# Score maxima of grouped-query attention on two halves of the array, and output weights split early and kept in DRAM

## The chip, the cores and the metric
The kernel runs on one core of one Trainium2 chip. The metric is the time of one execution on the device in microseconds (us), lower is better. The engines are TensorE (PE, with its weight loads as PEld), VectorE (DVE), ScalarE (ACT), GpSimd (POOL) and SyncE (SP), whose queue issues the transfers.

## The reference
One transformer layer over 1,024 tokens (a grid of 16 rows by 64 columns) of width 1,024, with 256 context tokens of which only keys and values are used. After a modulated RMS norm, a projection feeds three mixers: a long convolution (hyena, 256 wide), grouped-query attention (8 query heads on 2 key/value heads, 64 wide, over 1,024 + 256 keys) and attention in a neighbourhood of 8 by 16 (4 heads). Their outputs pass an output projection, and a gated feed-forward layer follows. All of it is float32. The part that matters here:

```python
q_l = apply_rope(rms_norm(q_l, qk_g_q[l]), cos, sin)
k_l = apply_rope(rms_norm(k_l, qk_g_k[l]), cos, sin)
gqa_l = gqa_latent(q_l, jnp.concatenate([k_c, k_l], axis=1), jnp.concatenate([v_c, v_l], axis=1))
    # in it: s = einsum(q, k) * ATTN_SCALE; p = softmax(s); o = einsum(p, v)
na_l = natten_latent(nq_l, nk_l, nv_l, nk_c, nv_c, na_rpb[l])
mix_l = jnp.concatenate([hyo_l, gqa_l, na_l], axis=-1) @ w_out[l]
```

## The kernel before
Every float32 operand of a product is split into a high and a low float16 part, and the product is made of high times high, high times low and low times high. The engines' programs are written by hand; the order of each engine's instructions is the order in the code, and semaphores join them. All transfers are issued by SP, in the order of its program.

**Projection stage.** 28 units (`UNITS`): 10 of kind 2 (neighbourhood keys and values), 10 of kind 1 (grouped-query keys and values, neighbourhood queries), 8 of kind 0 (grouped-query queries). `GROUP0[g]` is the first unit of a kind: 0, 10 and 20. For each unit TensorE runs `project(u)` and then `turn_qk(u - 2)`, the transposes of the unit two back. ScalarE reads the product (`from_psum`), makes the high parts (`hi_parts`) and copies the transposes (`turned`). VectorE runs `slot(u)`: mean square, rotation of unit u - 1, scaling of u (L2654, L2663), low parts of u - 1 (L2694), and then `meanwhile(u)`, which among others takes one row of the late modulation chunks (`late_row`, L2505) in each of the units 8 to 15. GpSimd makes the inverse roots (L1093). `turn_qk(u)` waits for the low parts of u (`pr_lo`). Weights arrive in chunks (`CHUNKS`) in four slots of 8 KB per partition; `load(c)` waits until the chunk that had the slot is used. Chunks 33 to 36 are the last four late ones, and follow chunk 32, the fourth of kind `qkv`. In the units 6 and 7 the hyena output is made and split (L2629, semaphore `y_rdy`, 4 in all).

**Neighbourhood stage.** 32 attention units, pipelined; among them the query units of kind 0 are projected, and the first eleven of the grouped-query maximum chunks (`early_chunk`) run in banks that are free for a while. The column of a query head in `qT` holds the high part in partitions 0 to 63 and the low part in 64 to 127; `kT[:, kv, 0]` holds the high part of the keys twice, `kT[:, kv, 1]` the low part and ones.

**Grouped-query stage.** 16 groups (8 blocks of 128 tokens by 2 key/value heads) of 10 steps, one for each tile of 128 keys. A step computes scores transposed, keys by 4 heads of 128 queries, with two matmuls of 512 columns (`step_scores`); the second takes `q2`, whose lower half is the high queries again (copied by GpSimd, `high_queries`, L1061) and whose upper half is the shift of each query, so that the exponential can be taken at once. ScalarE takes the exponential twice, as float16 (L2094) and as float32 (L2097); the difference is the low part, made by VectorE (L2810) for 6 tiles of a group and by GpSimd (L1077) for 4, for one of which GpSimd also makes the float16 part (L1075). Nine small matmuls weigh the values four steps later. For the shifts, a separate pass computes the plain scores of the group to come: 10 chunks (4 heads by 2 halves of the keys, and 2 for the context) of 512 columns, `chunk(c)` on all 128 partitions, one in each step, 13 steps ahead, in two banks by turns; VectorE takes the maximum of each (L2786), and at the tenth the negated maximum of all (L2799). TensorE moves it into place (`turn_shifts`, step 8) and ScalarE copies it (L2086).

```python
ps, k = PS[:, chunk_bank(c)], kT[:, c.kv, 0]
ins = mm(ps, qT[:, GROUP * c.kv + c.i // 2, tok(c.t)], k[:, o:o + 512], True, True)
```

**Output weights.** Four chunks of 1 MB, loaded during the neighbourhood and grouped-query stages; GpSimd scales them (L1047) and splits them (L1051, L1056), in pieces of 512 columns between its other work there. At the start of the grouped-query stage SP waits for the last neighbourhood unit (`o_mm`), then loads x again (3 MB), and, once the weights are split, eight blocks of 256 KB of the feed-forward weights. These loads so far start at 454.8 and later.

## Time and profile before
| | us |
|---|---|
| median of 3 runs | 1267.82 (1267.33 to 1268.02) |
| the profiled execution | 1269.27 |
| its span | 1267.5 |
| TensorE busy | 1242.6 (98%) |
| VectorE busy | 905.6 (71%) |
| ScalarE busy | 648.1 (51%) |
| GpSimd busy | 345.2 (27%) |

All times in the rows are us from the start of the span of the profiled execution. The projection stage reaches to about 293, the neighbourhood stage to about 388, the grouped-query stage to about 550. An engine's busy share is the mean over stages with different limits. An instruction's duration holds its way through the engine; what it costs in a stream is the distance to the next start.

### The profile page before, as it was taken

How to read it: one execution, taken by the hardware profiler on the slowest of the kernel's cores; microseconds unless marked ns; L12 is line 12 of the kernel's file. 1: busy time of each engine (PE TensorE's matmuls, PEld its weight loads, DVE VectorE, ACT ScalarE, POOL GpSimd, SP SyncE). 2: the span in 40 equal slices, each digit the busy share in tenths (PEclk: the TensorE clock that was granted, in tenths of full speed). 3: DMA queues.
4: the chain of work that ended last, by engine and by line, in shares of the span. 5: the costliest groups of instructions: out<-in, count | busy, mean ns of one | idle time of the engine just before them, and what ended most of it. 6: DMA issues, size and time to landing. Idle time of an engine off the chain costs nothing. (4 is left out here: it accounts for less than half of the span.)

```text
span 1267.5 us, 22616 instructions
## 1 busy us (share of the span) xinstructions
PE 1242.6 (98%) x7808; PEld 655.8 (52%) x7808; DVE 905.6 (71%) x1510; ACT 648.1 (51%) x1236; POOL 345.2 (27%) x341
## 2 busy tenths in 40 slices
PE   8999999999999999999999999999999999999997
PEld 1564656556675666664454444444444444444443
DVE  3879886766778999964458866666666675566587
ACT  2532224557779999973135654444454543312424
POOL 0100000114678899850003222333332220000001
PEclk9999999999999999999999999999999999999999
DMA  9628812335210120121130332222223305997963
GB/s 360 266 83 316 288 45 87 113 84 151 68 35 1 35 104 29 33 85 50 50 89 12 92 92 75 81 67 67 76 89 91 91 18 156 332 331 264 344 231 133
DMA packets 108164, 158.89 MB, mean 125 GB/s; under 512 B 8384, under 2 KB 67264, under 8 KB 106816
## 3 DMA queue, kind: packets, MB, share of 16 engines
q1 hardware_dynamic: 108096, 158.00, 36.8%
q8 instruction: 41, 0.67, 0.2%
q14 instruction: 27, 0.22, 0.1%
HBM read 135.95 MB, written 19.93 MB: 123 GB/s over the span
## 5 line engine op out<-in xcount | busy, mean ns | idle before, releaser
L1206 PE MATMUL PS<-arena 128*128 128x512 f16 (+9 forms) x7208 | 1201.1, 327 | 16.0 <-DMA arena<-in_w_mod 5.5
L1206 PEld LDWEIGHTS PS<-arena 128*128 128x128 f16 (+3 forms) x7208 | 604.7, 102 | 586.5 <-issue 39.5
L2894 DVE SCALAR_TENSOR_TENSOR arena<-arena 128x512 f16<-128x512 f32 x148 | 120.9, 823 | 76.6 <-ACT arena L2182 76.6
L2182 ACT ACTIVATE arena<-arena 128x512 f16<-128x512 f32 x140 | 87.6, 629 | 130.4 <-PE PS L1206 130.4
L2786 DVE TENSOR_REDUCE arena<-PS 128x1 f32<-128x512 f32 (+1 forms) x160 | 106.4, 680 | 9.1 <-PE PS L1206 9.1
L2294 ACT ACTIVATE arena<-arena 128x512 f16<-128x512 f32 x77 | 48.2, 629 | 123.3 <-DVE arena L3045 74.2
L2094 ACT ACTIVATE arena<-PS 128x512 f16<-128x512 f32 x140 | 88.3, 631 | 1.2 <-PE PS L1206 0.7
L1173 POOL TENSOR_TENSOR arena<-arena 128x512 f32<-128x512 f32 x20 | 26.6, 1334 | 222.2 <-DMA arena<-in_w_ffn_in 194.0
L1077 POOL TENSOR_TENSOR arena<-arena 128x512 f16<-128x512 f32 x64 | 74.1, 1159 | 9.4 <-ACT arena L2097 8.1
L1200 POOL TENSOR_TENSOR arena<-arena 128x1 f32<-128x1 f32 x8 | 4.7, 598 | 236.0 <-DVE arena L3186 236.0
L2810 DVE TENSOR_TENSOR arena<-PS,arena 128x512 f16<-128x512 f32 x96 | 65.4, 681 | 4.0 <-ACT PS L2097 3.9
L3060 DVE SCALAR_TENSOR_TENSOR arena<-arena 128x512 f16<-128x512 f32 x77 | 52.1, 686 | 20.2 <-ACT arena L2294 20.2
L2936 DVE TENSOR_TENSOR arena<-PS,arena 128x512 f32<-128x512 f32 x60 | 41.3, 688 | 32.4 <-PE PS L1206 31.2
L2097 ACT ACTIVATE PS<-PS 128x512 f32<-128x512 f32 x96 | 60.5, 632 | 0.0
L3045 DVE TENSOR_TENSOR arena<-arena 128x512 f32<-128x512 f32 x44 | 30.2, 690 | 37.7 <-DMA arena<-in_w_ffn_out 32.7
L2970 DVE TENSOR_TENSOR arena<-arena 128x512 f16<-128x512 f32 (+1 forms) x77 | 51.5, 683 | 0.0
L1119 POOL MEMSET arena<- 128x128 f16 x2 | 0.4, 205 | 181.7 <-PE PS L1460 181.7
L2245 ACT CAST arena<-arena 128x512 f16<-128x512 f32 (+1 forms) x77 | 44.9, 607 | 5.0 <-DVE arena L2977 2.9
L2217 ACT COPY arena<-PS 128x512 f32<-128x512 f32 x60 | 34.4, 576 | 18.4 <-PE PS L1206 18.4
L2097 ACT ACTIVATE arena<-PS 128x512 f32<-128x512 f32 x64 | 41.3, 646 | 0.0
L2222 ACT ACTIVATE arena<-arena 128x512 f32<-128x512 f32 x40 | 24.9, 623 | 28.3 <-DVE arena L2936 28.3
L2756 DVE CUSTOM_DVE_ANT_0 PS<-PS,arena 128x640 f32<-128x640 f32 x32 | 26.6, 831 | 16.9 <-PE PS L1206 16.4
(204 smaller groups left out, 1156.8 us busy)
## 6 DMA issues: line engine op xcount, KB each, us to landing
arena<-in_w_ffn_out SPq DMA_DIRECT2D x121, 256.0 KB, 5.1
arena<-in_w_mod SPq DMA_DIRECT2D x23, 1024.0 KB, 7.4
arena<-in_w_ffn_in SPq DMA_DIRECT2D x88, 256.0 KB, 3.0
arena<-in_w_in SPq DMA_DIRECT2D x9, 1024.0 KB, 5.5
left_operands<-arena SPq DMA_DIRECT2D x33, 256.0 KB, 2.2
arena<-left_operands SPq DMA_DIRECT2D x3, 2816.0 KB, 11.7
arena<-lay_bias SPq DMA_DIRECT2D x12, 512.0 KB, 4.0
arena<-in_x SPq DMA_DIRECT2D x2, 2048.0 KB, 13.9
```

The costliest lines, as they stand in the source:

```text
L1077: pool.tensor_tensor(pt[:, 1], Pf[s.full], pt[:, 0], ALU.subtract).then_inc(pt_lo2, 1)
L1206: return pe.matmul(out, lhsT, rhs, start=start, stop=stop, skip_group_check=True)
L2094: act.activation(Pt[s.s % RING_P][:, 0], PS[:, s.bank], ACT.Exp)
L2097: act.activation(Pf[s.full] if s.by_pool else PS[:, s.bank], PS[:, s.bank], ACT.Exp).then_inc(s_exp, 1)
L2182: act.activation(aS[n % RING][:, 0], weight_block(p, b), ACT.Copy, scale=WS).then_inc(blk_hi, 1)
L2245: act.copy(dst, f_op[name]).then_inc(fi_hi, 1)
L2294: act.activation(foS[q % FO_RING][:, 0], src, ACT.Copy, scale=WS).then_inc(fo_hi, 1)
L2786: dve.tensor_reduce(out, ps, AX, ALU.max).then_inc(s_max, 1)
L2810: dve.tensor_tensor(pt[:, 1], PS[:, s.bank], pt[:, 0], ALU.subtract).then_inc(pt_lo, 1)
L2894: dve.scalar_tensor_tensor(dst[:, 1], src, WS, dst[:, 0], ALU.mult, ALU.subtract).then_inc(blk_lo, 1)
L2970: dve.tensor_tensor(dst[:, 1], f_op[name], dst[:, 0], ALU.subtract).then_inc(fi_lo, 1)
L3060: dve.scalar_tensor_tensor(foS[q % FO_RING][:, 1], src, WS, foS[q % FO_RING][:, 0], ALU.mult, ALU.subtract).then_inc(fo_lo, 1)
```

## The change
1. **Maxima on half arrays, in pairs.** For odd heads `qT` now holds the low part in partitions 0 to 63 and the high part in 64 to 127. The maximum pass takes the high queries alone: one head on partitions 0 to 63, the other on 64 to 127, as two matmuls of 64 rows into two banks (`Pair`, five a group, one in every second step, banks 4 and 5 each time). VectorE takes one maximum over 1,024 columns for a pair. The first ten chunks, in the neighbourhood stage, stay single, on one half each; the eleventh goes.
2. **Shifts.** The negated maximum is split into a float16 part and its rest: three dependent VectorE instructions in place of one.
3. **High queries by transfer.** Since odd heads have them in the other half, SP issues two transfers a group in place of GpSimd's copy: groups 0 and 1 during the bias loads, the others after the loads of the feed-forward blocks.
4. **Tiles.** GpSimd makes the low part of 5 tiles of a group in place of 4, and the float16 part of 3 in place of 1.
5. **Output weights.** Eight pieces of 512 KB are loaded, scaled by GpSimd, split by ScalarE (high) and GpSimd (low), 1,024 columns an instruction, one in each unit from 11 on, and stored in DRAM; at the start of the grouped-query stage they are loaded back, 4 MB, ahead of x. The fourth late modulation sum moves in two steps to make room.
6. TensorE's loop over the groups is written out.

```diff
-LEAD, LAG, SHIFT_AT, SEND_AT = 13, 4, 8, 4
+LAG, SHIFT_AT, SEND_AT, LEAD = 4, 8, 4, 6
-RING_P, RING_F = 5, 4
-POOL_TILES, CAST_TILE, LAST_CASTS = (1, 4, 6, 8), 4, (0, 3, 5, 7)
-CHUNK_BANK, STEP_BANK, OUT_BANK = (5, 1), (0, 2, 4, 3), (6, 7)
+RING_P, RING_F = 5, 5
+POOL_TILES, CAST_TILES, LAST_CASTS = (1, 3, 5, 7, 9), (1, 3, 7), (0, 4, 8)
+NPAIR_G = 5
+PAIR_BANK, STEP_BANK, OUT_BANK = (4, 5), (0, 2, 1, 3), (6, 7)
...
+    def pairs(self):
+        if self.s < 2:
+            return [Pair(NPAIR_G + self.s)] if self.s else []
+        return [Pair(self.s // 2 + LEAD, self.it)] if self.s % 2 == 0 and self.s // 2 + LEAD < NGROUP * NPAIR_G else []
...
+        def query_heads(kv, h, t):
+            rows = slice(HD * (h % 2), HD * (h % 2) + HD)
+            return qT[rows, GROUP * kv + h, tok(t)], kT[rows, kv, 0]
...
+            def load_wo(h):
+                k, n = 4 * (h // 4) + 2 * (h % 2), h // 2 % 2
+                sp.dma_start(wo_raw[h % 2], w_out[:, k:k + 2, 512 * n:512 * n + 512]).then_inc(wo_raw_in[h % 2], 16)
+            def keep_wo(h):
+                sp.wait_ge(wo_split, h + 1)
+                if h + 2 < N_WO:
+                    load_wo(h + 2)
+                sp.dma_start(wo_kept[:, h // 2, :, 2 * (h % 2):2 * (h % 2) + 2], wo_parts[h % 2])\
+                    .then_inc(wo_out[h % 2], 16)
...
                     load(c, w_in[:, kh:kh + 4, col:col + 512], (4, 512))
+                if c == chunk_index("qkv", 3):
+                    sp.wait_ge(y_rdy, 4)
+                    for h in range(2):
+                        load_wo(h)
...
+            def high_queries(g):
+                s = Step(NKT * g)
+                if g >= 2:
+                    sp.wait_ge(st_mm, NKT * (g - 1))
+                for b in range(2):
+                    high = qT[HD * b:HD * b + HD, GROUP * s.kv + b:GROUP * s.kv + GROUP:2, tok(s.t)]
+                    dst = q2[s.kv][0:HD].rearrange("p (h b t) -> p h b t", b=2, t=P)[:, :, b]
+                    sp.dma_start(dst, high).then_inc(q2_hi[s.kv], 16)
...
             sp.wait_ge(o_mm, NNA)
+            sp.wait_ge(pr_r, n_normed(NU - 1))
+            for n in range(4):
+                sp.dma_start(woS[n], wo_kept[:, n]).then_inc(wo_in, 16)
             for i in range(3):
                 sp.dma_start(x1[:, 2 * i:2 * i + 2], x_rows[:, 2 * i:2 * i + 2]).then_inc(x1_in, 16)
...
             for b in range(2):
-                sp.wait_ge(wo_split, 3 + b)
                 for a in ("A11", "A12", "A21", "A22"):
                     load_fi(a, 0, b)
+            sp.wait_ge(pr_tc, NU)
+            for g in range(2, NGROUP):
+                high_queries(g)
...
+            def wo_scale(h):
+                pool.wait_ge(wo_raw_in[h % 2], 16 + 16 * (h // 2) + 16)
+                r = flat(wo_raw[h % 2])
+                pool.tensor_scalar(r, r, WS / HS if h in (0, 2) else WS, None, ALU.mult).then_inc(wo_scaled, 1)
+            def wo_low(h):
+                pool.wait_ge(wo_hi, 3 + h + 1)
+                pool.tensor_tensor(flat(wo_parts[h % 2][:, 1]), flat(wo_raw[h % 2]), flat(wo_parts[h % 2][:, 0]),
+                                   ALU.subtract).then_inc(wo_split, 1)
...
                 inverse_roots(u)
+                h = u - GROUP0[1] - 1
+                if h >= 1:
+                    wo_low(h - 1)
+                if 0 <= h < N_WO:
+                    wo_scale(h)
...
+            def pair(p):
+                if p.p == NPAIR_G:
+                    pe.wait_ge(pr_n, n_normed(NU - 1))
                     pe.wait_ge(pr_tc, NU - 1)
                 else:
+                    pe.wait_ge(s_max, n_paired(p) - 1)
+                for o in range(2 if p.i == NPAIR_G - 1 else 1):
+                    for b in range(2):
+                        if p.i == NPAIR_G - 1:
+                            q, k = query_heads(p.kv, 2 * o + b, p.t)
+                            ins = mm(PS[:, PAIR_BANK[b], C * o:C * o + C], q, k[:, S:S + C], True, True)
+                        else:
+                            q, k = query_heads(p.kv, 2 * (p.i // 2) + b, p.t)
+                            ins = mm(PS[:, PAIR_BANK[b]], q, k[:, 512 * (p.i % 2):512 * (p.i % 2) + 512], True, True)
                 ins.then_inc(s_mm, 1)
...
+            def wo_high(h):
+                act.wait_ge(wo_scaled, 3 + h + 1)
+                if h == 1:
+                    act.wait_ge(late_used, 24 + LATE_MOVE + 1)
+                elif h >= 2:
+                    wo_stored(act, h - 2)
+                act.copy(flat(wo_parts[h % 2][:, 0]), flat(wo_raw[h % 2])).then_inc(wo_hi, 1)
...
-                dve.tensor_reduce(maxima, mx[:, c.kv], AX, ALU.max, negate=True).then_inc(sh_rdy, 1)
+                dve.tensor_reduce(lowest, mx[:, c.kv], AX, ALU.max, negate=True).then_inc(sh_rdy, 1)
+                dve.wait_ge(sh_rdy, 3 * c.g + 1)
+                dve.tensor_copy(maxima, lowest).then_inc(sh_rdy, 1)
+                dve.wait_ge(sh_rdy, 3 * c.g + 2)
+                dve.tensor_tensor(rest_of_maxima, lowest, maxima, ALU.subtract).then_inc(sh_rdy, 1)
```

## Rows read from the trace of the kernel before

**Rows 1.** Busy time of each engine in three stretches, number of instructions, granted clock, transfers.
```profile
core 0: us, PE busy (x) PEld busy (x) DVE busy (x) ACT busy (x) POOL busy (x), PEclk, DMA share, GB/s
250.00:260.00 10.00, 10.00 (x54) 4.80 (x53) 6.98 (x23) 7.25 (x15) 1.39 (x2) 1.00 0.01 3
340.00:360.00 20.00, 19.91 (x232) 14.39 (x230) 15.71 (x40) 15.00 (x36) 13.52 (x12) 1.00 0.19 54
460.00:480.00 20.00, 19.61 (x239) 12.94 (x236) 18.63 (x35) 19.90 (x41) 18.94 (x21) 1.00 0.54 210
```
**Rows 2.** TensorE's timeline, grouped-query stage: start, length, what, wait before.
```profile
410.98 1.18 PE L1206 MATMUL PS<-arena 128*128 128x512 f16 x12 [0.19 <-ACT arena L2086]
...
454.27 10.41 PE L1206 MATMUL PS<-arena 128*128 128x512 f16 x126 [0.20 <-ACT arena L2086]
464.86 10.39 PE L1206 MATMUL PS<-arena 128*128 128x512 f16 x126 [0.18 <-ACT arena L2086]
```
**Rows 3.** VectorE's timeline, two score maxima in a row.
```profile
467.89 1.29 DVE L2786 TENSOR_REDUCE arena<-PS 128x1 f32<-128x512 f32 x2
```
**Rows 4.** TensorE's timeline, filter taps on 64 rows (L1206) between transposes (L1276).
```profile
42.25 1.12 PE L1206 MATMUL PS<-arena 64*128 64x512 f32 x2
43.30 0.66 PE L1276 MATMUL PS<-arena 128*128 128x128 f32 x4
43.89 1.39 PE L1206 MATMUL PS<-arena 64*128 64x512 f32 x4
45.21 0.66 PE L1276 MATMUL PS<-arena 128*128 128x128 f32 x4
```
**Rows 5.** Groups of instructions by shape, 15 to 62, float32 passes of 512 columns.
```profile
L1206 PE MATMUL PS<-arena 128*2 128x512 f32 x50 | 22.1, 592 | 0.0
```
**Rows 6.** TensorE's timeline, projection stage: a turn, and a unit's product.
```profile
235.21 0.61 PE L1460 MATMUL PS<-arena 128*128 128x128 f16 x8
...
238.72 5.34 PE L1206 MATMUL PS<-arena 128*128 128x512 f16 x24
```
**Rows 7.** VectorE's timeline, units 7 to 9.
```profile
229.69 1.31 DVE L2629 TENSOR_TENSOR arena<-arena 128x512 f16<-128x512 f32 x1 [0.19 <-ACT arena L1965]
...
231.76 0.74 DVE L2518 TENSOR_SCALAR arena<-arena 128x1024 f32<-128x1024 f32 x1
233.03 0.43 DVE L2654 SCALAR_TENSOR_TENSOR arena<-PS,arena 128x256 f16<-128x256 f32 x1 [0.53 <-ACT arena L1987]
233.54 0.69 DVE L2694 TENSOR_TENSOR arena<-arena 128x512 f16<-128x512 f32 x1
```
**Rows 8.** SP's timeline: the four late chunks, first to last issue.
```profile
203.31 13.98 SPq L811 DMA_DIRECT2D arena<-in_w_mod  x4
```
**Rows 9.** Transfers by line, us to landing: the first, and the last two, of these.
```profile
arena<-in_w_mod SPq DMA_DIRECT2D x1, 1024.0 KB, 5.1
...
arena<-in_w_mod SPq DMA_DIRECT2D x2, 1024.0 KB, 8.2
```
**Rows 10.** Groups by shape, GpSimd, 220 to 560: busy, mean ns, idle before.
```profile
L1077 POOL TENSOR_TENSOR arena<-arena 128x512 f16<-128x512 f32 x64 | 74.1, 1159 | 9.4 <-ACT arena L2097 8.1
L1047 POOL TENSOR_SCALAR arena<-arena 128x512 f32<-128x512 f32 x16 | 23.8, 1494 | 0.0
...
L1075 POOL CAST arena<-arena 128x512 f16<-128x512 f32 x16 | 9.8, 615 | 9.7 <-ACT arena L2097 9.7
```
**Rows 11.** GpSimd's timeline, the last query's rotation.
```profile
391.05 1.27 POOL L1109 TENSOR_TENSOR arena<-arena 128x512 f32<-128x512 f32 x1
```
**Rows 12.** What TensorE waited for, 420 to 430: total, times, longest.
```profile
PE PS L1206 <- POOL arena L1077: 1.0, 1, 1.0
```
**Rows 13.** Transfers by line, us to landing: issues from 1123.4 to 1124.8.
```profile
arena<-left_operands SPq DMA_DIRECT2D x1, 2816.0 KB, 10.0
...
arena<-in_w_ffn_out SPq DMA_DIRECT2D x1, 256.0 KB, 11.8
```
**Rows 14.** TensorE's timeline, its last matmuls.
```profile
1251.78 8.37 PE L1206 MATMUL PS<-arena 128*128 128x512 f16 x38
```
**Rows 15.** Busy time and granted clock (0.76) after them.
```profile
1264.00:1265.00 1.00, 0.00 (x0) 0.00 (x0) 0.00 (x0) 0.00 (x0) 0.00 (x0) 0.76 1.02 379
```

More of the change, by code:

```diff
@@ L74, in n_split @@
 def n_split(c):
-    return sum(k not in AS_IS and k != "wo" for k in CHUNKS[:c + 1])
+    return sum(k not in AS_IS for k in CHUNKS[:c + 1])
 STEPS = [(p, b) for p in ("P2", "P1", "P5", "P6", "P7", "P3", "P4") for b in range(2)]
@@ L818, in _ @@
             n_of["mod"] = 1
-            for c in range(1, N_EARLY):
+            for c in range(1, len(CHUNKS)):
                 if c == 1:
@@ L1618, in step @@
                 step_scores(s)
-                for c in s.chunks():
-                    chunk(c)
+                for p in s.pairs():
+                    pair(p)
                 if s.turns_shifts():
@@ L1674, in _ @@
             weigh(Unit(NNA - 1))
-            for s in range(3, BODY):
+            for s in range(3, NSTEPS):
                 step(Step(s))
@@ L2007, in turned @@
                 if g == 0:
+                    if t == 0:
+                        for h in range(N_WO - 2, N_WO):
+                            wo_stored(act, h)
                     ins = act.copy(qT[:, :, tok(t)], ps)
@@ L2816, in step @@
             def step(s):
-                for c in s.chunks():
-                    chunk_maximum(c)
+                for p in s.pairs():
+                    pair_maxima(p)
                 if s.s:
```

231 lines of the change are left out of this document (108 added, 123 removed).

## The prediction
> **What bounds the kernel now.** I read the windows first, one for each stage that the change touches [rows 1]. Where TensorE is busy throughout, a microsecond by which it is late is, as a rule, a microsecond of the kernel. In the projection stage (250 to 260) TensorE is full, VectorE and ScalarE have some 30% free and GpSimd does almost nothing. In the neighbourhood stage (340 to 360) TensorE is full but for 0.09 of 20 us. In the grouped-query stage (460 to 480) ScalarE is as full as TensorE, VectorE has 7% left and GpSimd 5%.
>
> Then the timeline of TensorE in that last stage: a beat of 10.59 us for each group of ten steps (454.27 to 464.86), with one wait of 0.2 us at its start, for the shifts that ScalarE copies at L2086 [rows 2]. The reader is to see that both engines run at their limit: ScalarE has 21 instructions a group, 0.50 each, and is busy for 19.90 of 20 us; TensorE is idle only where it waits for ScalarE. A 512-column matmul costs it 0.216 us in a stream ((5.34 - 0.38) / 23, where 0.38 is the length of one, in [rows 6]). The wait and the restart behind it leave 10.24 us of its own work in a group. VectorE starts its 512-column instructions 0.61 apart (1.29 for two of 0.68) [rows 3]: 16 of them are 9.8 us, plus small ones. ScalarE sets the beat; TensorE and VectorE are a few per cent behind.
>
> **The change, part by part.**
> *Grouped-query steps.* ScalarE loses two float16 exponentials a group, 0.50 each: 10.6 - 1.0 = 9.6 us. TensorE loses ten 512-column matmuls (2.16 us) and gets five pairs at P each. VectorE has 5 low parts (3.0), 5 maxima over 1,024 columns and some more small ones. Two 512-column ones end to end are 1.22, so I take 1.15 each, with one start in place of two, and 0.8 for the shift's chain of three and the reciprocal: 9.6 us. GpSimd has 5 low parts at 1.16, 3 casts at 0.61 and the outputs (some 1.2), in place of a scaling or two, a split and a copy more than it keeps: 8.8 us [rows 10]. Everything hangs on P. The trace has no float16 matmul on 64 rows; the nearest are the float32 taps [rows 4]. A float32 pass of 512 columns costs about 0.43 (22.1 us for 50, 0.44) [rows 5]. Two passes on one half, from 42.25 to the next start at 43.30, take 1.05, where streaming wants 0.86. The four passes of 128 columns behind them take 0.59 to the next start, where 0.44 is the stream (0.11 each, a quarter of 0.43). So one visit to the half array costs 0.19 + 0.15 = 0.34 us beside its work. Four passes, two on each half, take 1.32 where one half alone would need 1.72: the halves do overlap, the second adding 0.27 to the first's 1.05. For float16, whose weights are half as wide, I take 0.22 for the stream, 0.05 for the second half's later start and 0.23 for the two changes of shape, P = 0.50, between 0.40 (0.18 of changes only) and 0.65 (all 0.34 and some weight loading). A group is then 10.24 - 2.16 + 2.5 + 0.1 (the two semaphore waits at its start remain) = 10.7 on TensorE, 0.1 more than now: the saving of two heads at once goes into changing shape ten times a group. Over 15 groups +1.5 us, from -6 (P 0.40) to +13 (0.65).
> The Trainium skill's page "TensorEngine Tiling (Array Packing)", section "Key Properties", says that a change of tiling mode, not just of tile, drains TensorE. It gives no price; the 0.34 us of the taps is what a drain each way looks like here.
>
> *Early chunks, neighbourhood stage.* Ten of them now run on one half each. Each costs a visit (0.2 to 0.34) and saves nothing; TensorE is full there, less a wait of 0.25 in every four units that can absorb some. Chunk 10 leaves (0.22). +1.2 us (0 to +3).
>
> *The weights' loads ahead of the projection stage.* The queue of SP now waits, behind the load of the fourth projection chunk, until the hyena output is split, and only then goes on to the four late modulation chunks. That split ends at 231.0 (229.69 + 1.31, [rows 7]). Now the four are issued from 203.3 to 217.3 [rows 8], and the first is read at 231.76, 0.8 us after the point where its load may start in the new kernel. Ahead of it go two loads of 512 KB. A 1 MB load lands 5.1 us after issue on an empty queue, and a fourth in a row after some 9 (8.2 is the median of the last two), so each MB adds 2 to 2.6, of which I take 2.6 [rows 9]. 231.1 + 5.1 + 2.6 = 238.8: VectorE stands 7.0 us at L2518. Queued behind it are the scaling (L2654) and low part (L2694) of the units that follow; now they end 1.2 us after the one at 233.03 begins [rows 7]. In the new order they end at 238.8 + 0.7 + 1.2 = 240.7, and TensorE's turn of that unit, now at 235.21 [rows 6], waits for them: 5.5 us. TensorE is full before and after, so nothing gives it back. I take +5.7 (4 to 7).
>
> *Splitting on GpSimd and ScalarE.* GpSimd gets a scaling and a subtraction over 1,024 columns in each of eight units. From 1.49 and 1.16 for 512 [rows 10]: 2.95 + 2.25, plus the inverse root of 0.70 (1.39 for two in [rows 1]) and about 0.5 of waiting for ScalarE's high part between them, 6.4 us. A unit lasts 5.6 (24 matmuls and the turn of 0.61, less overlap, [rows 6]). GpSimd falls 0.8 us further behind in each of some seven units, to 5.5; what waits for its inverse root (scaling, low parts, turn) has some 2.5 of slack. +3 us (0 to 5).
>
> *GpSimd in the grouped-query stage.* The extra weight work in the third group, for which TensorE waited 1.0 us [rows 12], goes: -1.0. The cast of tile 1 now stands ahead of the last low parts of the queries: +0.6, but inside the stall that follows. Copying the high queries on GpSimd goes too, off the path.
>
> *High queries by DMA.* Groups 0 and 1 are loaded early. Those of group 2 are queued on SP behind everything that now starts at about 392.4, when the last query is rotated (391.05 + 1.27, [rows 11]) and the last unit weighed: 4 MB of split weights, 3 MB of x and eight quarter blocks, 9 MB. At 5.1 for the first MB and 2.6 for each further one they have landed after 25.9 us, at 418.4, and the small loads just behind. Is it one line? A load of 2,816 KB took 10.0 us, and one of 256 KB issued a microsecond behind it took 11.8 [rows 13], where 1 MB on an empty queue takes 5.1 [rows 9]: yes. Group 2 begins at 410.98 [rows 2]. TensorE stands for 419 - 411 = 8 us with ScalarE and VectorE behind it, less the 0.6 above. +7.5 (5 to 10). Group 3 finds its queries landed.
>
> *The clock.* Nothing in the middle of this kernel is long enough to show it; at the end the last matmul is done at 1260.2 (1251.78 + 8.37, [rows 14]) and the granted clock still averages 0.76 from 1264 to 1265, so that it falls from 2.4 to 1.2 GHz some 4.3 us after the last matmul [rows 15]. Two stalls of 5.5 and 7.5 may each be followed by some us at 1.2 GHz. +1 (0 to 4).
>
> Sum: 1.5 + 1.2 + 5.7 + 3 - 1 + 7.5 + 1 = 18.9 us. The profiled execution took 1269.27 us (span 1267.5), 1.45 over the median of 1267.82. 1288.2 on its basis, **1286.7** on that of the median.
>
> **Rivals.**
> *The halves cost no change of shape.* Then P is 0.22 to 0.27, TensorE has 9.3 us a group, and VectorE and ScalarE set the beat at 9.6: -1.0 in each of 15 groups in place of +0.1, 16.5 us less: 1270. For it: the overlap in [rows 4], and the gaps there stand beside float32 weights and waits for VectorE. Against: every one of the changes seen has them. The Trainium skill's page "TensorE: Matmul & The Clock Gate", section "Measured speedup vs the span model", has packed tiles take one matmul plus about 4 ns for each further tile, which would be this rival; the 0.27 of the second half here is more.
> *A load does not block.* If the high queries pass the 9 MB, or those land in a third less time, 7.5 us go: 1279. If the late chunks' rows are not the gate: 1281. Against it the 11.8 us.
> *Faster than before.* The first rival together with the absence of one of the two stalls, say the queries in time: 1286.7 - 16.5 - 7.5 = 1262.7. It decides where P is under 0.27 and group 2 is not kept waiting more than 4 us.
> *Worse.* P at 0.65 or over: 1298 and more.
>
> **How the numbers follow.** My forecast with both stalls and P near 0.50 has 0.50 (its own range 1280 to 1294). One stall missing 0.13, the halves free with both stalls 0.14, both (faster) 0.17, P high 0.06. A change within 0.2%, 2.5 us, is about what a measurement cannot tell from none: 0.04 of the cases end there. Faster 0.16, same 0.04, slower 0.80. The range from 1268 to 1298 leaves out the faster cases and the worst.
>
> **What would show it.** In the new profile: a hole of about 7 us in VectorE before the first late row (now L2518), released by a DMA, and one of 5.5 in TensorE; TensorE's beat at 10.6 to 10.8 us, with gaps around each pair; the two matmuls of a pair starting within 0.06 us; a hole of some 8 us at the start of group 2, released by the DMA of the high queries; ScalarE no longer full. I am wrong if the beat is 9.6 to 9.8, if the first pair follows its neighbours without a gap, or if either hole is missing.

## The result and the profile after

The changed kernel takes 1304.09 us (median of 4 runs, 1303.27 to 1304.67), the kernel before, measured beside it, 1267.62: a ratio of 1.0287, 95% interval 1.0269 to 1.0305, slower by 36.5 us. The profiled execution took 1304.67 us, its span is 1302.9, 35.4 more than before. 1286.7 was forecast, 1268 to 1298 the range. The sign was right, and both stalls and the beat of a group came where they were expected; the loss was twice the size that was forecast.

The windows of the changed kernel in the three stretches of [rows 1]:

```profile
250.00:260.00 10.00, 10.00 (x54) 4.76 (x53) 7.27 (x16) 4.45 (x11) 7.55 (x8) 1.00 0.60 185
340.00:360.00 20.00, 19.82 (x217) 13.53 (x214) 15.16 (x41) 13.93 (x35) 10.83 (x10) 1.00 0.22 61
460.00:480.00 20.00, 19.07 (x238) 10.87 (x239) 18.71 (x27) 18.56 (x37) 15.86 (x20) 1.00 0.04 8
```

ScalarE is no longer full, as forecast. But no engine is full in the last stretch: something small is waited for in each group.

To see where 35.4 us come from, I put the two traces side by side at fixed points of TensorE's order (the transposes of a unit, the scores of a step) and took the difference, less the difference at unit 7, which lies ahead of every edit. The same for some of the experiments told below, in us behind the kernel before:

```
point                  after    e1     e2     e3     e5    e10    e16
unit 9                   8.0   0.0    8.7    7.3    7.4    0.0    0.0
unit 17                 15.1   7.1   13.1   14.4   10.3    0.0    0.0
unit 19                 16.8   8.8   19.5   16.1   13.4    4.6    4.6
unit 25                 20.2  14.2   22.1   18.3   18.6    7.9    5.5
step 18 (group 1)       22.2  15.8   24.3   20.2   20.8    7.8    5.6
step 28 (group 2)       33.6  28.0   35.4   20.4   32.1    7.8    5.4
step 38                 32.6  27.1   34.4   19.4   31.1    6.6    4.1
step 140                34.6  29.1   36.4   21.4   33.2    6.5    3.1
last matmul             35.5  30.0   37.3   22.3   34.1    7.5    3.3
```

The first column is the account of the loss: 8.0 to unit 9, 8.8 in units 11 to 19, 3.4 in the neighbourhood stage, 2.0 in the first steps, 11.4 at group 2, 1.0 given back in group 3, 2.0 in the groups behind it, 0.9 at the end. Some 6.7 us of it are TensorE's clock, which fell four times; they are told below.

The first hole, on VectorE's timeline, then TensorE's (the same places before: [rows 6, 7]):

```profile
239.09 0.75 DVE L2581 TENSOR_SCALAR arena<-arena 128x1024 f32<-128x1024 f32 x1 [7.34 <-DMA arena<-in_w_mod]
```
```profile
240.83 1.03 PE L1498 MATMUL PS<-arena 128*128 128x128 f16 x8 [5.53 <-DVE arena L2757]
```

7.0 and 5.5 were forecast. The turn behind it takes 1.03 us, not 0.61. The windows say why:

```profile
236.00:238.00 2.00, 0.00 (x0) 0.00 (x0) 0.00 (x0) 0.00 (x0) 0.00 (x0) 1.00 1.02 387
238.00:239.00 1.00, 0.00 (x0) 0.00 (x0) 0.00 (x0) 0.00 (x0) 0.00 (x0) 0.90 1.02 418
239.00:240.00 1.00, 0.00 (x0) 0.00 (x0) 0.92 (x2) 0.00 (x0) 0.00 (x0) 0.50 1.04 430
...
244.00:245.00 1.00, 1.00 (x6) 0.75 (x5) 1.00 (x2) 0.00 (x0) 0.00 (x0) 0.50 1.05 410
245.00:246.00 1.00, 1.00 (x8) 0.76 (x7) 0.32 (x1) 0.00 (x0) 0.00 (x0) 0.69 0.97 385
246.00:247.00 1.00, 1.00 (x14) 0.84 (x12) 0.27 (x1) 0.45 (x2) 0.11 (x1) 1.00 1.05 393
```

TensorE stops at 235.3; the granted clock falls to half (1.2 GHz) from about 238.8 (a mean of 0.90 in 238 to 239) and stays there until about 245.6 (0.69), nearly five us into the new work. That costs another 2.3 us.

The second hole, SP's timeline and TensorE's:

```profile
414.00 1.94 SPq L960 DMA_DIRECT2D arena<-split_output_weights  x4
415.98 1.56 SPq L962 DMA_DIRECT2D arena<-in_x  x3
417.58 20.59 SPq L967 DMA_DIRECT2D arena<-in_w_ffn_in  x8
438.27 2.54 SPq L924 DMA_DIRECT2D arena<-arena  x4
```
```profile
442.54 3.85 PE L1242 MATMUL PS<-arena 128*128 128x512 f16 x24 [9.04 <-DMA arena<-arena]
```

The high queries of group 2 are the last line of SP: they are not even issued before 438.27, since issuing eight loads of 256 KB took SP 20.59 us behind 7 MB. Another 2.3 us go to the clock here too: it is down from 436.8 to 447.0, 4.5 us into the new work.

The clock fell twice more, and no long hole stands before these falls. The first comes behind the turn of unit 16: TensorE's next 46 matmuls in the changed kernel, then in run 6 below, whose program is the same up to the grouped-query stage, then the granted clock of the changed kernel:

```profile
291.04 9.33 PE L1242 MATMUL PS<-arena 128*128 128x1 f32 x46
```
```profile
291.12 7.65 PE L1242 MATMUL PS<-arena 128*128 128x1 f32 x46
```
```profile
293.00:294.00 1.00, 1.00 (x8) 0.53 (x7) 0.58 (x2) 1.00 (x4) 0.86 (x1) 0.71 0.68 147
294.00:295.00 1.00, 1.00 (x4) 0.34 (x3) 1.00 (x1) 0.70 (x3) 1.00 (x1) 0.50 1.02 338
...
413.00:414.00 1.00, 1.00 (x18) 0.91 (x17) 1.00 (x2) 0.00 (x0) 1.00 (x1) 0.50 0.00 0
```

The clock is at 1.2 GHz from 293.4 to 296.8, with TensorE at work, and costs 1.7 us (9.33 less 7.65). In the ten us before, TensorE had stood twice, for 1.23 and 1.16 us. Run 6 stands for 1.15 us in the same place and keeps its clock, so that one execution has such a fall and another has not. The fourth fall, from 412.9 to 416.3, follows waits of 1.26, 1.70 and 0.79 us in the first steps of the grouped-query stage. There other waits take up most of it: run 1, which has no fall there, loses 1.6 us from unit 25 to step 18, the changed kernel 2.0.

Units 11 to 19, where the largest miss lies; VectorE and GpSimd in unit 14:

```profile
274.01 2.53 DVE L2757 TENSOR_TENSOR arena<-arena 128x128 f16<-128x128 f32 x2 [0.44 <-ACT arena L2044]
```
```profile
273.09 2.13 POOL L1115 TENSOR_TENSOR arena<-arena 128x1024 f16<-128x1024 f32 x1
275.19 2.81 POOL L1111 TENSOR_SCALAR arena<-arena 128x1024 f32<-128x1024 f32 x1
```

The two low parts of the keys took 0.63 together before (0.29 and 0.42, one behind the other):

```profile
268.65 0.63 DVE L2694 TENSOR_TENSOR arena<-arena 128x128 f16<-128x128 f32 x2 [0.38 <-ACT arena L2000]
```

Now the first ends at 275.37, when GpSimd's subtraction ends (275.22), and the second takes 1.25 beside the next. GpSimd meanwhile is idle 1.4 to 1.6 us a unit: it is not behind, as I had it; it is in the way. The Trainium skill, "SBUF — State Buffer", section "Who interferes with whom", has the rule: VectorE and GpSimd share a pair of ports under an exclusive lock; a VectorE instruction with two inputs in SBUF is blocked by a GpSimd instruction that reads SBUF until that one ends, one with a single input is not, and some copies and scalings take the pair too. The trace agrees, with 0.63 against 2.53. Of the 8.8 us, 1.7 are the fall of the clock at 293.4; 7.1 are left.

The grouped-query stage, TensorE [rows 2] and the chain it waits for:

```profile
464.46 10.28 PE L1242 MATMUL PS<-arena 128*128 128x128 f16 x126 [0.47 <-DVE arena L2877]
475.21 0.96 PE L1242 MATMUL PS<-arena 128*128 128x128 f16 x14 [0.47 <-DVE arena L2877]
```
```profile
474.14 0.17 DVE L2873 TENSOR_REDUCE arena<-arena 128x4 f32<-128x12 f32 x1
474.34 0.26 DVE L2875 CAST arena<-arena 128x4 f16<-128x4 f32 x1
474.51 0.61 POOL L1125 CAST arena<-arena 128x512 f16<-128x512 f32 x1
...
474.63 0.52 DVE L2877 TENSOR_TENSOR arena<-arena 128x4 f16<-128x4 f32 x1
```

The beat is 10.75 us. A pair: the last full matmul ahead of one starts at 476.80, both halves at 477.11 (0.003 apart), the next full one at 477.43: 0.63, less 0.22 for the full one, P = 0.42 us. And a subtraction on four columns takes 0.52: it ends at 475.15, with GpSimd's cast (475.12).

### The profile page after: what moved, and what is told of

It is laid out like the page before. It is cut to its first block, busy times and chain, and to the rows that moved or that the text cites. A ratio compares the mean times of both kernels' runs of the same rounds, so it can differ in the third digit from the quotient of the medians.

```text
span 1302.9 us, 22186 instructions
## 1 busy us (share of the span) xinstructions
PE 1252.1 (96%) x7808; PEld 641.5 (49%) x7808; DVE 920.6 (71%) x1450; ACT 646.7 (50%) x1213; POOL 362.4 (28%) x341
## 4 chain that ended last, share of the span: by engine, by line
PE 61%; DVE 8%; issue 2%; SPq 2%; ACT 2%; POOL 1%; DMA 1%; another core or an unknown queue 0%; DVEq 0%; POOLq 0%; ACTq 0%
PE PS L1242 59%; SPq L967 2%; DVE arena L2862 1%; PE PS L1560 1%; DMA arena<-weight_sum_rows 1%; DVE arena L3207 1%; DVE arena L3210 1%; DVE arena L3087 1%; DVE arena L2969 1%; PE PS L1312 1%; ACT arena L2397 1%; POOL arena L1127 1%; DVE arena L3077 1%; DVE arena L2877 0%; ACT arena L2055 0%
## 5 line engine op out<-in xcount | busy, mean ns | idle before, releaser
L1242 PE MATMUL PS<-arena 128*128 128x512 f16 (+10 forms) x7208 | 1209.3, 329 | 32.2 <-DMA arena<-arena 9.0
L1242 PEld LDWEIGHTS PS<-arena 128*128 128x128 f16 (+4 forms) x7208 | 590.6, 102 | 625.1 <-issue 47.3
L2862 DVE TENSOR_REDUCE arena<-PS 128x2 f32<-128x1024 f32 (+1 forms) x75 | 91.6, 1222 | 20.1 <-PE PS L1242 17.7
L1127 POOL TENSOR_TENSOR arena<-arena 128x512 f16<-128x512 f32 x80 | 92.4, 1156 | 23.9 <-ACT arena L2154 20.1
L2151 ACT ACTIVATE arena<-PS 128x512 f16<-128x512 f32 x109 | 65.7, 603 | 18.5 <-PE PS L1242 18.1
L2888 DVE TENSOR_TENSOR arena<-PS,arena 128x512 f16<-128x512 f32 x80 | 54.4, 680 | 3.7 <-ACT PS L2154 3.6
L2154 ACT ACTIVATE arena<-PS 128x512 f32<-128x512 f32 x80 | 47.7, 597 | 3.2 <-PE PS L1242 1.6
L2154 ACT ACTIVATE PS<-PS 128x512 f32<-128x512 f32 x80 | 48.7, 609 | 0.0
L2579 DVE SCALAR_TENSOR_TENSOR arena<-arena 128x1024 f32<-128x1024 f32 x28 | 36.6, 1309 | 3.4 <-DMA arena<-in_w_mod 1.6
```

The lines of the kernel that those rows point to most:

```text
L1127: pool.tensor_tensor(pt[:, 1], Pf[s.full], pt[:, 0], ALU.subtract).then_inc(pt_lo2, 1)
L1242: return pe.matmul(out, lhsT, rhs, start=start, stop=stop, skip_group_check=True)
L2151: act.activation(Pt[s.s % RING_P][:, 0], PS[:, s.bank], ACT.Exp)
L2154: act.activation(Pf[s.full] if s.by_pool else PS[:, s.bank], PS[:, s.bank], ACT.Exp).then_inc(s_exp, 1)
L2862: dve.tensor_reduce(out, ps, AX, ALU.max).then_inc(s_max, 1)
L2888: dve.tensor_tensor(pt[:, 1], PS[:, s.bank], pt[:, 0], ALU.subtract).then_inc(pt_lo, 1)
```

## The experiments

Medians of 4 to 7 runs; single runs of one kernel spread by up to 7 us, so differences under 2 us are read from the table and the traces, not from medians. The clock has a part in the spread: the traces of runs 1, 3, 4, 5, 8 and 11 have a fall of 3.4 us near 136, ahead of every edit, and the others have none there. The table leaves that one out, since it counts from unit 7, but not the later ones. Ratios are to the kernel before.

**1. Late chunks first.**

```diff
-                if c == chunk_index("qkv", 3):
+                if c == chunk_index("qkv", 4) - 1:
                     sp.wait_ge(y_rdy, 4)
```

> The changed kernel with one edit: the queue of SP issues the last four late modulation chunks before it waits for the split hyena output, so their loads start some 15 us earlier; the two first loads of the output weights stay behind that wait. Theory (the queue's order starves VectorE): the hole of 5.5 us in TensorE at 235.3 and the 2.3 us that its unit 9 loses at the lower clock behind it both go, the span is 8.0 us shorter, 1296 us. Rival (something else holds the late row, or the hole moves on to the next chunk of weights): at least 4 of the 8 us stay, 1300 or more. If the clock's 2.3 us were not due to the hole they would stay too: 1298.5.

1297.56 us (1.0226, 1.0209 to 1.0243). The hole and the clock's 2.3 us are gone at unit 9, exactly 8.0 us. Of these 2.0 are lost again by unit 25. 1.4 of them go between units 20 and 21, where the clock is down from 320.4 to 323.8 in this run and not in the changed kernel; the other 0.6 go between units 19 and 20, where ScalarE stands for something that the trace does not name. Its waits in the neighbourhood stage (293 to 400), in the changed kernel and here:

```profile
ACT arena L2138 <- remote: 2.7, 1, 2.7
```
```profile
ACT arena L2138 <- remote: 3.3, 1, 3.3
```

The kernel before has no such line; 16 of the 17 kernels derived from the changed one have one, of 1.2 to 4.3 us on ScalarE; run 17 has none. It is open below.

**2. ScalarE does not wait for GpSimd's scaling.**

```diff
-                act.wait_ge(wo_scaled, 3 + h + 1)
+                act.wait_ge(wo_raw_in[h % 2], 16 + 16 * (h // 2) + 16)
...
-                act.copy(flat(wo_parts[h % 2][:, 0]), flat(wo_raw[h % 2])).then_inc(wo_hi, 1)
+                act.activation(..., ACT.Copy, scale=WS / HS if h in (0, 2) else WS).then_inc(wo_hi, 1)
```

> The changed kernel with one edit: ScalarE makes the high part of the output weights from the loaded rows by itself (it scales as it copies) and waits for no one but the load; GpSimd scales and subtracts as much as before, later in the unit. Two theories for the 8.8 us that units 11 to 19 lose. Loop theory (ScalarE waits for GpSimd's scaling, the high parts of keys behind it are late, so VectorE's row and TensorE's turn): without that wait the units are back at 5.6 us, 1295.5 us. Port theory (VectorE's low parts of the keys, 0.29 and 0.42 us alone, take 1.43 and 1.25 beside a scaling or subtraction of GpSimd): GpSimd works as long as before, so the two rows of VectorE stay near 1 us or more each and at least 5 of the 8.8 us stay, 1300 to 1304.

1306.09 us (1.0298, 1.0281 to 1.0315), units 11 to 19 lose 10.7 instead of 8.8: the loop theory, by which they would lose nothing, falls. But the port theory's own sign is only half met: the low parts are back at 0.68 for two. The victim has changed. VectorE's scaling of two columns (0.17 us elsewhere) now meets GpSimd's subtraction, and ends with it (279.85):

```profile
278.11 1.78 DVE L2701 TENSOR_SCALAR arena<-arena 128x2 f32<-128x2 f32 x1
```
```profile
276.88 2.97 POOL L1113 TENSOR_TENSOR arena<-arena 128x1024 f16<-128x1024 f32 x1
```

GpSimd pays as well, 2.97 in place of 2.13, behind VectorE's late rows. The 10.7 us are not all the port's: in this run ScalarE also waits 10.5 us for the stores of the split weights (262 to 300), and the clock is down from 300.5 to 307.4. Up to unit 17, ahead of that fall, 4.4 us are lost, where the changed kernel without its own fall loses 5.4.

**3. Queries between the loads.** SP's order at the end of the neighbourhood stage: queries of group 2, 4 MB of weights, group 3, x, group 4, four blocks, group 5, four blocks, the rest.

> The changed kernel with one edit: the copies of the high queries of groups 2, 3, 4 and 5 stand between the loads of the output weights (4 MB), x (3 MB) and the blocks of the first layer (2 MB) in SP's queue, where they stood behind all of them. Theory (the queue of loads keeps group 2's queries): the hole of 9.2 us at 433 and the 2.3 us at the lower clock behind it go, less what GpSimd's casts had still to catch up: 1304.1 - 11 = 1293. Rival (GpSimd, or the weighing of the last neighbourhood unit, is the gate, the queries land early anyway): no more than 3 us are gained, 1301. Second rival: the hole moves to group 3 or 4, whose queries now follow 4 MB or 3 MB: 3 to 6 us stay, 1296 to 1299.

1292.88 us (1.0194, 1.0177 to 1.0211), 11.2 less. In the table group 2 costs 0.2 in place of 11.4, and no later group is kept waiting by a load.

**4. No half of the array.**

```diff
-            rows = slice(HD * (h % 2), HD * (h % 2) + HD)
+            rows = slice(0, P)
```

> The changed kernel with one edit: every matmul of the maximum pass, early chunks and pairs, uses all 128 rows (high and low parts of the queries against the high keys), so that no half of the array is ever used and the two heads of a pair follow one another. Theory (a pair costs 0.417 us: one stream of 0.216 and 0.20 for two changes of shape, so that it saves next to nothing against two streams of 0.432): the beat of a group goes from 10.75 to 10.82 us, +1.1 over 15 groups, and the ten early chunks give back 0.1 each: 1304 within 1.5 us. Rival (the two halves at once save a whole stream a pair, 0.216, and the rest of the beat is a wait): 75 pairs cost 16 us more, 1320. Rival (the changes of shape cost more than the stream saves): 1300 or less.

1304.29 us (1.0276, 1.0259 to 1.0293): the same time. The beat is 10.86, 0.11 more. Between units 21 and 24 TensorE no longer falls behind (0.00 a unit, where the change loses 0.42 for two early chunks). So a visit to one half costs 0.21 us, and a pair saves 0.02.

**5. GpSimd out of the weights' split.** Experiment 2's ScalarE edit, and on VectorE, at the end of each unit from `GROUP0[1] + 2`:

```diff
+            def wo_low(h):
+                dve.wait_ge(wo_hi, 3 + h + 1)
+                dve.scalar_tensor_tensor(flat(wo_parts[h % 2][:, 1]), flat(wo_raw[h % 2]),
+                                         WS / HS if h in (0, 2) else WS, flat(wo_parts[h % 2][:, 0]),
+                                         ALU.mult, ALU.subtract).then_inc(wo_split, 1)
```

> The changed kernel with one edit: GpSimd no longer touches the output weights; ScalarE makes the high part (scaling as it copies) and VectorE the low part (scale and subtract in one instruction of 1.2 us, as its late rows), at the end of each unit. Port theory (VectorE's low parts of the keys stood still beside GpSimd's weight work): they are back at 0.29 and 0.42 us, a unit back at 5.4 to 5.7 us although VectorE does 1.2 us more in it, units 11 to 19 lose at most 1.5 of the 8.8 us, 1295.5 to 1297. Rival (the whole of the weight work is too much for the stage, whoever does it): VectorE, 70% busy before, becomes the limit, units stay at 6.5 us or more, 1301 or more.

1301.4 us (1.0257, 1.024 to 1.0274). The low parts are back:

```profile
273.70 0.63 DVE L2743 TENSOR_TENSOR arena<-arena 128x128 f16<-128x128 f32 x2 [0.57 <-ACT arena L2029]
```

Units 11 to 17 lose 2.8 where the change loses 7.1, and 1.7 of each are a fall of the clock: 1.1 against 5.4, though VectorE does 1.2 us more in each. But most of it is gone by unit 25: ScalarE now stands for something that GpSimd's slowness had hidden, the stores of the split weights. Of ScalarE's waits, 262 to 300:

```profile
ACT arena L2086 <- DMA split_output_weights<-arena: 10.3, 5, 4.6
```

**6. Shifts after the weighing**: on TensorE `step_weigh` ahead of `turn_shifts`.

> The changed kernel with one edit: in the step where the shifts of the next group are transposed, TensorE first weighs the values of that step (0.57 us) and then transposes, so that VectorE's chain of three small instructions, whose last takes 0.52 us beside a cast of GpSimd, is done by then. Theory (the wait of 0.47 us at each group's shifts is the only thing in which TensorE, 10.2 us of work, is late): the beat goes from 10.75 to 10.25 or 10.3 us, 14 groups give 6.5 us, 1297.5. Rival (ScalarE's copy of the shifts then comes too late for the first step of the next group, or VectorE with its 10.05 us a group takes the limit at once): the beat stays at 10.6 or more, 1302 or more.

1304.01 us (1.0274, 1.0257 to 1.0291), the beat 10.57: 0.17 us of the wait came back. The chain's subtraction still ends with GpSimd's cast (477.86 and 477.82), and TensorE stands twice, 0.17 us each, for it and for the maximum behind it. The 2.4 us that 14 groups give back do not show in the median. In the trace they do (36.9 us behind at step 28, 36.7 at the last matmul, where the changed kernel goes from 33.6 to 35.5), but the clock is down from 324.6 to 331.4 in this run and not in the changed kernel, and takes as much (2.5 us lost from unit 20 to 21, 0.4 in the changed kernel).

**7, 8. The edits 1, 3, 5 and 6 together, and with them the early chunks on all rows.**

> The changed kernel with the edits of the late loads, of the queries' copies between the loads, of the output weights' split on ScalarE and VectorE, and of the shifts after the weighing, all together. If the four losses are separate, they add: 7.2 + 11.2 + 8.8 + 6.5 = 33.7 us less than 1304.1, 1270.4. If one hides behind another (TensorE, once early, waits for the bias tables' loads or for GpSimd): 1274 or more. If removing stalls lets the queries' group or VectorE gain more: 1267.

> As the run with the four edits, and the ten early chunks of the maximum pass in the neighbourhood stage use all 128 rows, while the pairs stay on the two halves. An early chunk on one half costs 0.20 us for its two changes of shape and saves nothing: 10 of them, 2.0 us less than with the four edits alone, 1268.4. Rival (other waits of the stage take it up): no difference, within 0.5 us.

1279.59 (1.0096, 1.0079 to 1.0113) and 1280.17 us (1.0096, 1.0074 to 1.0118). 24.5 of the 33.7 us: not separate, since ScalarE waits 10.4 us for stores here too. The early rows do stop the loss of 0.42 a unit; the median does not show 2 us, the traces 1.7 at the last matmul (9.9 and 8.2 behind).

**9, 10, 11. On top: the high part last in ScalarE's unit; then the first pairs at steps 2, 3, 5, 6; then all pairs on 128 rows.**

> As the run with the four edits and the early rows, and ScalarE makes the high part of the output weights after the high parts of the keys and the copies of the turned tiles, at the end of its unit. Theory (in units 15 to 19 ScalarE stands 10.4 us in all before that copy, until the store of the split weights two halves earlier has landed, and holds up the keys behind it): the keys no longer wait, TensorE has back 2 to 5 of the 5.9 us that it is behind at unit 19, 1275 to 1278. Rival (ScalarE's wait only moves to the next unit's copies out of PSUM, or the copies of the near values gate the next stage anyway): less than 1 us, 1279.5 to 1280.5.

> As the run before it, and the first pairs of the maximum pass come at steps 2, 3, 5 and 6 in place of 1, 2, 4 and 6. Theory (at steps 0 to 3 TensorE waits 2.5 us for VectorE's maxima over 1,024 columns, because all pairs use the same two banks and three of them follow one another within 4 us): 1 to 2 us less than the run with the high part last. Rival (VectorE has its work to do in those steps in any order): no difference within 0.5 us.

> As the run with the pairs spread, and all pairs on 128 rows, so that no half of the array is used anywhere. By the rate of the first such run (0.10 us a group) it is 1.5 us slower than that run, within 1 us. If, with the stalls gone, VectorE alone sets the beat, no difference; if TensorE's switching costs more than it shows, up to 2 us faster.

1277.67 (1.0077, 1.006 to 1.0094), 1274.35 (1.0046, 1.0031 to 1.0061) and 1279.31 us (1.0082, 1.0066 to 1.0099). The first steps lose nothing now (table, e10, unit 25 to step 18). With the stalls gone the halves are worth something: the beat is 10.58 with them and 10.79 without, 0.21 us a group.

**12. The kernel before, with work on GpSimd that nobody uses**, in six units, on a scratch buffer (its results go nowhere):

```diff
                 inverse_roots(u)
+                if GROUP0[1] + 1 <= u <= GROUP0[1] + 6:
+                    extra = f32(104, 1024)
...
+                    own.step(pool.tensor_tensor(extra, extra, extra, ALU.subtract))
+                    own.wait()
+                    own.step(pool.tensor_scalar(extra, extra, 1.0, None, ALU.mult))
```

> The kernel before with work added that nobody uses: in six units of the projection stage (12 to 17) GpSimd, behind its inverse root, subtracts and then multiplies 1,024 columns in a scratch buffer (2.2 and 2.8 us). No wait is added but that the next inverse root comes behind it, which has 5 us to spare. Port theory: VectorE's low parts of the keys, 0.29 and 0.42 us now, take 1.2 us or more each where they fall beside it, and each of the six units is 0.6 to 1.3 us longer: 1268 + 4 to 8 = 1272 to 1276. Rival (the 8.8 us came from the waits between the engines and the stores, not from the port): both rows keep their length, 1268 to 1269.

1272.63 us (1.0032, 1.0021 to 1.0044), 4.0 us behind at unit 17 and 3.7 at the last matmul, with no fall of the clock before that. VectorE before, VectorE here, and GpSimd beside it:

```profile
245.98 0.28 DVE L2694 TENSOR_TENSOR arena<-arena 128x128 f16<-128x128 f32 x1
```
```profile
247.95 1.77 DVE L2703 TENSOR_TENSOR arena<-arena 128x128 f16<-128x128 f32 x1
249.64 2.13 DVE L2525 SCALAR_TENSOR_TENSOR arena<-arena 128x1024 f32<-128x1024 f32 x1
```
```profile
247.68 1.89 POOL L1130 TENSOR_TENSOR arena<-arena 128x1024 f32<-128x1024 f32 x1
249.66 2.78 POOL L1132 TENSOR_SCALAR arena<-arena 128x1024 f32<-128x1024 f32 x1
```

0.28 becomes 1.77 (ending 249.72, GpSimd's 249.57), with no semaphore between the two. That is the collision without the weights, their loads and their stores. One wait came with it: VectorE stood once, 2.4 us, for the inverse root of the first of these units, which GpSimd reached late.

**13. The chain's maxima in PSUM** (on top of 10):

```diff
+        lowest_ps = PS[:, PAIR_BANK[0], 0:GROUP]
...
-                    query_shifts(p)
+                    query_shifts(p, lowest_ps)
...
+                if p.i == 0 and p.p > NPAIR_G:
+                    pe.wait_ge(sh_rdy, 3 * p.g)
```

> As the run with the pairs spread, and VectorE keeps the four maxima of a group in PSUM (in a bank that the pairs use) in place of SBUF, so that the chain's copy and subtraction read PSUM; TensorE's first pair of a group waits for the chain. Port theory: the chain's copy and subtraction, 0.26 and 0.52 us beside GpSimd's cast, take 0.18 each as where GpSimd rests (0.18 and 0.18 in the first group), TensorE's two small waits of 0.17 us a group go, the beat is 10.57 - 0.34 = 10.23 us, 4.5 to 5 us less: 1269.5. Rival (VectorE's own work, 10.05 us a group, or ScalarE sets the beat anyway): the beat is 10.5 or more, 1273 or more.

1278.17 us (1.008, 1.006 to 1.01). VectorE's subtraction with one input in SBUF, beside the same cast:

```profile
478.81 0.61 POOL L1122 CAST arena<-arena 128x512 f16<-128x512 f32 x1
...
478.85 0.18 DVE L2880 TENSOR_TENSOR arena<-PS,arena 128x4 f16<-128x4 f32 x1
```

0.18, not 0.52: the mechanism holds. The beat is 10.74 all the same, since the wait that I had added stands ahead of a pair and costs 0.46.

**14, 15. VectorE's low part one unit later (on top of 10), and both.**

> As the run with the pairs spread, and VectorE makes the low part of each half of the output weights one unit later, so that it no longer stands (1.4 and 1.8 us) for ScalarE's high part, which waits for the stores of the split weights. Theory: the first neighbourhood unit and, behind it, the copies of the last near values start 1.5 to 2 us earlier, TensorE is 2 to 4 us less late there: 1271. Rival (the stores behind the near values' copies just make the next high part late instead): less than 1 us.

> The two edits together. If both theories hold they add: 1274.4 - 5 - 3 = 1266, 1 to 3 us faster than the kernel before, which would be what two heads at once are worth when nothing else is made later by it. If only the chain's does: 1269.5. If neither: 1274.

1288.78 (1.0154, 1.0137 to 1.017) and 1289.72 us (1.0163, 1.0143 to 1.0183): wrong by 18 and 24 us, and 14 to 15 slower than run 10. The ring of split weights has two places; a later low part is a later store, and in run 14 ScalarE waits 13.8 us for stores between 262 and 300 (1.9 in run 10). The stalls bring the clock down four times between 281 and 333, for 17.1 us in all (once, for 3.4, in run 10). By an estimate that can be up to half of the loss: half of the 13.7 us more at 1.2 GHz, against 12.2 us more by unit 25.

**16, 17, 18. In the chain's step TensorE weighs, transposes, then scores the pair (on top of 13); stores and loads of the output weights issued on ScalarE's queue (on top of 10); both.**

> As the run with the chain in PSUM, and in the step where the chain falls TensorE weighs first, then transposes the shifts, then scores the pair (which was put ahead of the weighing and waited 0.5 us for the chain); VectorE makes that step's low part before the pair's maxima. Port theory: nothing waits for the chain any more, the beat falls from 10.75 to 10.2 or 10.3 us, 1269 to 1270. Rival (VectorE's 10.05 us a group, now in a worse order, sets it): 10.5 or more, 1274 or more.

> As the run with the pairs spread, and the loads of the next halves of the output weights and the stores of the split ones are issued on ScalarE's DMA queue in place of SP's, where they stood among the copies of the near values (7 us of issuing). Theory (ScalarE's high parts wait for stores, 10.4 us in one of the runs, because the stores are late in SP's queue, and so the last keys, the first neighbourhood unit and the last near values are late): the 7 us by which TensorE is behind at unit 20 fall to 2 or less, 1269. Rival (the stores are slow by themselves, or the near values' copies, some 17 us from issue to landing, are the gate): at least 5 of the 7 stay, 1272 or more.

> The edits of the two runs together. If both theories hold: 1274.4 - 4.5 - 5 = 1265, 2 to 4 us faster than the kernel before. If one of them: 1269 to 1270, slower than before by 1 us.

1273.55 (1.004, 1.0025 to 1.0056), 1275.06 (1.005, 1.0035 to 1.0066) and 1272.75 us (1.0031, 1.002 to 1.0042). The beat falls to 10.48 and TensorE is full:

```profile
460.00:480.00 20.00, 19.96 (x241) 11.48 (x242) 18.33 (x28) 18.99 (x37) 16.61 (x20) 1.00 0.03 7
```

So 10.2 was up to 0.3 too low for TensorE's own work, and the gain of the idea over the old 10.59 is 0.11 us a group, under 2 us in all. By the measure of the table run 17 is 3.9 us behind at unit 20 where run 10 was 7.6, but nearly all of the difference arises between units 19 and 20: at unit 19 they are 4.0 and 4.6 behind. Between these units run 10 has ScalarE's nameless waits (3.5 and 0.9 us) and a fall of the clock at 310.2, and run 17 has neither. So the stores' place in the queue is shown to be worth 0.6 us; whether the nameless wait went with it is not shown. No version beats the kernel before.

## Why the prediction was wrong in size

The forecast was 18.9 us, the profile has 35.5: 16.6 are missing. Two terms left their own bounds by most: the clock (5.7 us missing) and the splitting of the weights (4.1).

**Late loads: right.** 7.34 and 5.53 us for 7.0 and 5.5, and 5.7 of TensorE's time for 5.7; experiment 1 gives the 8.0 back, clock included.

**Splitting on GpSimd and ScalarE: a step that failed, 7.1 us for 3 (8.8 with the clock).** The step reads: "GpSimd falls 0.8 us further behind in each of some seven units". It priced GpSimd as a queue of its own, 6.4 us of work in a unit of 5.6. Its work is 5.6 and it rests in each unit. What the runs showed in its place is that VectorE's instructions on SBUF stand while it works: by taking GpSimd out (run 5), by moving the collision on to another victim (run 2), and by making it in the kernel before (run 12). The loss lay outside the bounds of 0 to 5, which were made from GpSimd's durations alone. That it is VectorE beside GpSimd is shown by runs 5 and 12; that the two share ports is the Trainium skill's explanation, which no run contradicts.

**Early chunks, 3.4 for 1.2.** Ten visits at 0.21 are 2.1 (run 4); I had the visit right (0.2 to 0.34) and took off more for waits that would absorb some. The rest, 1.2, comes between units 19 and 20, where the nameless wait of ScalarE lies: not foreseen. The first steps lose another 2.0 (0.4 of it the clock), also not foreseen: pairs 5, 6 and 7 use the same two banks within four us and wait for VectorE's maxima of 1.2 us each; spreading them took it away (run 10).

**High queries: right mechanism, 9.0 for 7.5 to 8**, and experiment 3 gives back all of the group's 11.4. I had them queued behind 9 MB, landing behind them; they were not even issued until 438.27, when SP had issued the last of the eight blocks.

**The clock: the other step that failed, 6.7 us for 1, outside 0 to 4.** The step reads: "Two stalls of 5.5 and 7.5 may each be followed by some us at 1.2 GHz." There were four falls and not two: 2.3, 1.7, 0.4 and 2.3 us. The stretch at 1.2 GHz lasted well into the work behind each of the two holes (4.8 and 4.5 us), which nothing in the trace of the kernel before could show, since there the only fall stands at its end. And the step looked for long stalls alone ("Nothing in the middle of this kernel is long enough to show it"), where two falls followed waits of 0.8 to 1.7 us each. These come in one execution and not in another (run 6), so a part of this term is chance.

**Grouped-query steps: 2.0 for 1.5, by two errors that cancel.** P is 0.42 and not 0.50 (five pairs, 0.4 us a group less), the lower end of my range. In its place came the chain of the shifts, which I had in VectorE's sum as work and not on TensorE's path, lengthened beside GpSimd's cast (0.52 for 0.18 in its last instruction, run 13). 10.7 was forecast, 10.75 came. The Trainium skill's rule that a change of tiling mode drains TensorE ("TensorEngine Tiling (Array Packing)", "Key Properties") is borne out, by 0.10 us on either side of a pair; so is, for the pair itself, the few ns for a second tile of "TensorE: Matmul & The Clock Gate", here 0.003. The rival built on the latter left out the former.

**GpSimd's wait in the third group: right,** -1.0. At the end of the stage 0.9 us are lost that I did not follow up.

Of the forecast's signs, both holes, the beat and ScalarE's free time were as written, and still the total was half the true one: the terms had been found by following waits, and neither a conflict without a semaphore nor a slower clock is in a chain of waits. The one rival that reached 1298 and more had a high P as its cause; P came out low.

What stays open: ScalarE's wait that the trace calls remote, which none of the runs was made for. In the changed kernel ScalarE stands there (L2138) for the semaphore of TensorE's weighing (`o_mm`); the last matmul of the weighing is recorded to end at 321.5, its semaphore arrives at 324.2, and what keeps it is not shown. In the changed kernel and its nearest relatives the loss between units 19 and 20 goes with the length of the wait: 0.0 at 1.6 us (run 3), 1.2 at 2.7 (the changed kernel), 1.6 at 3.1 (run 4), 1.8 at 3.3 (run 1). Open too is whether a third place in the ring of split weights would take the rest of the neighbourhood stage's late start away, which was not tried. In run 18 unit 20 is still 4.3 us behind.

## What to carry to other kernels

Work given to an idle GpSimd is not free because GpSimd has time: look at what VectorE does on SBUF in the same microseconds, above all with two operands there, and who waits for that (in run 2 it was a scaling of two columns); reading one of the operands from PSUM (run 13), or taking the work off GpSimd (run 5), takes the conflict away. Here each of the two long stalls of TensorE cost its own length and 2.3 us more at half clock, and repeated waits of a microsecond or two brought the clock down as well in some executions; before a difference of two or three us between two runs is explained, their granted clocks are to be compared. When loads are added to a queue, count also the small copies and stores behind them: here they were not even issued for 20.6 us, and mending one stall shows the next that it had covered (24.5 of 33.7 us here).

## What the runs showed of the hardware

- A VectorE instruction on 2 or 4 columns took 1.78 and 0.52 us beside a GpSimd instruction, 0.17 and 0.18 without; with its first operand in PSUM 0.18 beside it. The collision lengthens GpSimd's too (2.97 for 2.13).
- Two float16 matmuls on two halves start 0.003 us apart, and each change between half and full array costs about 0.10 us: two heads at once cost 0.42 against 0.43 one after the other.
- At the two holes, of 5.5 and 9.0 us, the clock fell 3.5 and 3.3 us after TensorE's last matmul and came back 4.8 and 4.5 us after its next: 2.3 us each. It also fell with no wait over 1.7 us in the ten us before, and the same 46 matmuls then took 9.33 us, not 7.65.
- Issuing eight loads took SP 20.6 us when 7 MB were on their way.
